# Sparse stage of the sample group: which input positions share a product, the order in which gathered rows lie, and when the value weights and the last pairs' chains are taken

## The reference, cut to what matters

```python
def compress_blocks(kv, pos_emb, w1, w2):
    # block i covers rows [i*16, i*16+32)
    hid = silu(einsum('nilgd,ldf->nigf', blocks + pos_emb, w1))   # 32 rows x 64 -> 256
    return einsum('nigf,fd->nigd', hid, w2)
...
# the compressed probabilities, summed over heads, choose the blocks
o = gates[..., 0] * o_cmp + gates[..., 1] * o_sel + gates[..., 2] * o_win
```

## Time and profile before

| | |
|---|---|
| median of 3 runs | 1810.35 us (1809.63 to 1811.09) |
| the profiled execution's own time | 1798.39 us |
| its span, first to last instruction | 1796.4 us |
| mean granted TensorE clock | 0.983 |
| the stage's PE products (L3329) | 980.2 us to 1253.9 us |

### The profile page before, as it was taken

How to read it: one execution, slowest core, us unless ns; L and a number is a source line. 1 busy time by engine, 2 the same in 40 slices (tenths; PEclk the granted TensorE clock), 3 DMA queues, 4 the chain that set the end, 5 groups by cost and what they waited for, 6 DMA issues and landing times. The chain is left out here.

```text
span 1796.4 us, 35438 instructions
## 1 busy us (share of the span) xinstructions
PE 1707.8 (95%) x13591; PEld 1427.7 (79%) x13591; DVE 964.7 (54%) x2741; ACT 732.3 (41%) x1582; POOL 425.8 (24%) x597
## 2 busy tenths in 40 slices
PE   7999999899898999999998987999799999999998
PEld 6778878678775878877788876988688888888998
DVE  5322222387455545221225878777587877778534
ACT  5200000276332424000112435445687777787513
POOL 0000000000464000000004434231365656565300
PEclk9999999999999999999999998999899999999999
DMA  6353343464888675575336434346400000000254
GB/s 222 133 176 135 140 170 110 159 210 126 288 248 269 241 249 174 134 201 184 131 108 207 150 119 129 125 148 167 119 20 26 26 25 20 25 14 8 58 161 156
DMA packets 150973, 247.47 MB, mean 138 GB/s; under 512 B 35451, under 2 KB 85368, under 8 KB 148504
## 3 DMA queue, kind: packets, MB, share of 16 engines
q1 hardware_dynamic: 135496, 200.58, 34.7%
q0 software_dynamic: 7424, 33.56, 5.4%
q10 hardware_dynamic: 7888, 11.08, 2.2%
...
## 5 line engine op out<-in xcount | busy, mean ns | idle before, releaser
L2000 POOL TENSOR_SCALAR sparse_pr<-sparse_pr,sparse_coef,sparse_gate 128x63 f32<-128x63 f32 (+8 forms) x384 | 246.8, 666 | 162.4 <-DVE sparse_coef L1940 162.4
L1886 ACT ACTIVATE sparse_pr<-sparse_pr,sparse_nmax 128x63 f32<-128x63 f32 (+8 forms) x384 | 227.7, 595 | 69.0 <-DVE sparse_nmax L1934 68.8
L1247 PE MATMUL x_acc<-x_w_hi,x_y_lo 128*128 128x512 f32 (+3 forms) x448 | 157.2, 351 | 1.7 <-DVE x_y_lo L1059 1.5
L1247 PE MATMUL x_acc<-x_w_lo,x_y_hi 128*128 128x512 f32 (+3 forms) x448 | 155.3, 347 | 0.0
L1247 PE MATMUL x_acc<-x_w_hi,x_y_hi 128*128 128x512 f32 (+3 forms) x448 | 155.0, 346 | 0.0
L512 PE MATMUL h_acc<-h_w_hi,h_y_lo 128*128 128x512 f32 x384 | 151.7, 395 | 0.8 <-DVE h_y_lo L434 0.8
L512 PE MATMUL h_acc<-h_w_lo,h_y_hi 128*128 128x512 f32 x384 | 150.1, 391 | 0.0
L512 PE MATMUL h_acc<-h_w_hi,h_y_hi 128*128 128x512 f32 x384 | 149.8, 390 | 0.0
L459 DVE COPY cmp_w<-h_acc 128x512 f32<-128x512 f32 x48 | 33.2, 691 | 204.7 <-PE h_acc L512 204.7
L1807 PE MATMUL sparse_ps<-cmp_lent,ss_pieces 64*128 64x384 f32 (+3 forms) x928 | 138.6, 427 | 3.9 <-DVE sparse_part L1934 2.2
L1819 PE MATMUL sparse_ps<-constants_shared,sparse_pr 128*128 128x128 f32 x1120 | 132.8, 276 | 3.4 <-DVE sparse_nmax L1934 2.3
...
## 6 DMA issues: line engine op xcount, KB each, us to landing
...
```

Of the source, the lines that this page charges most:

```text
L1247: last = nc.tensor.matmul(acc[b][:, 0:passes[p][3]], left[:, k, t * P:(t + 1) * P], weights(right, p)[:, k, :], start=(k == 0 and a == 0), ...
L1886: nc.scalar.activation(row, row, ACT.Exp, scale=-1.0, bias=nmax[u % UB][:, e * NBR + br:e * NBR + br + 1], accum_out=lsum[u % UB][:, e * N ...
L2000: nc.gpsimd.tensor_scalar(row, row, one, gate[:, t, 2 * i + e, (br + 1) % 3:(br + 1) % 3 + 1], ALU.mult, ALU.mult).then_inc(scaled, 1)
```

## The change

It does five things.

1. `SHARED` is steps 0 to 5 rather than 1 to 6, so an item begins with shared steps and ends with the two others; the first slot of an item forms the `ps_x` products first and waits for the addition to `ps_h[0]` behind them, and the wait for `ps_h[1]` stands behind three more.
2. Within 32 partitions the quarter gather now brings the rows of even positions first, then those of odd ones. The transposes of `turn_x` then write runs of 16 neighbouring values instead of alternating between the even and the odd half of the row. The index table is loaded by 8 small DMAs for each part instead of 4.
3. Value weights: the ring has 2 buffers with a third column block for the sum, so that POOL's sum waits for no cut; the parts are taken at slots 3, 5, 8, 10, 13, 15 of item 3 and 2, 4 of item 4, before at 3, 5, ..., 15 and (4,1); the sums of parts 0 and 1 are made in item 2.
4. The chains of pair 2 hang 4 slots earlier, those of pair 3 8 slots earlier; "cmp" of the pairs starts at (1,3), (2,4), (4,3), (5,8), before at (1,3), (2,4), (4,4), (6,4). In each chain "psel", "pwin", "values" and "acc" stand one slot later behind "scale" than before.
5. At the start of the stage DVE prepares step 0 behind the low part of the summed weights and the queries, before ahead of them.

```diff
-    SHARED = (1, 2, 3, 4, 5, 6)
-    RING_W = 3
+    SHARED = (0, 1, 2, 3, 4, 5)
+    RING_W = 2
...
     for p in range(PAIRS):
+        moved = max(0, p - 1) * 4
+
+        def slot(n, hh):
+            return divmod(n * HALVES + hh - moved, HALVES)
         e, o = 2 * p, 2 * p + 1
...
-        cmp_item, c0 = (o, 3) if p == 0 else (e, 4)
+        n, c0 = ((1, 3), (2, 4), (4, 3), (5, 8))[p]
...
+        for x, what in enumerate(("mask", "exp", "coef", "scale")):
+            at(*slot(o, tail + x), what, p)
         for x in range(2):
-            turn_at(*later(6), "psel", p, x)
-            turn_at(*later(7), "psel", p, 2 + x)
-        turn_at(*later(8), "pwin", p, 0)
-        turn_at(*later(8), "pnew", p, 0)
-        at(*later(10), "values", p)
-        at(*later(11), "acc", p)
+            turn_at(*slot(o, tail + 7), "psel", p, x)
+            turn_at(*slot(o, tail + 8), "psel", p, 2 + x)
+        turn_at(*slot(o, tail + 9), "pwin", p, 0)
+        turn_at(*slot(o, tail + 9), "pnew", p, 0)
+        at(*slot(o, tail + 11), "values", p)
+        at(*slot(o, tail + 12), "acc", p)
...
+    def weights_turn(n, hh):
+        at = [3 + 5 * l // 2 for l in range(KD)]
+        x = (n - PAIRS + 1) * HALVES + hh
+        return at.index(x) if x in at else None
...
-                last = nc.vector.transpose(to.rearrange("p r (n j) -> p n j r", n=8), fr.rearrange("p q g d -> p g q d"))
+                last = nc.vector.transpose(to.rearrange("p r (n j) -> p n r j", n=8), fr.rearrange("p q g d -> p g q d"))
...
-                    if sum_at(l):
-                        pool.wait_ge(next_cut, SHARED[sum_at(l) - 1] + 1)
-                    nc.gpsimd.tensor_tensor(w_next_sum[:, :], w_next[l % RING_W][:, 0, :], w_next[l % RING_W][:, 1, :], ALU.add).then_inc(next_summed, 1)
+                    nc.gpsimd.tensor_tensor(w_next[l % RING_W][:, 2, :], w_next[l % RING_W][:, 0, :], w_next[l % RING_W][:, 1, :], ALU.add).then_inc(next_summed, 1)
...
-                    if n == PAIRS - 1 and hh >= 2 and hh % 2 == 0 and shared(hh // 2 - 1):
-                        next_sum(hh // 2 - 1)
+                    if n == PAIRS - 2 and hh < RING_W and shared(hh):
+                        next_sum(hh)
+                    l = weights_turn(n, hh + 1)
+                    if l is not None and l >= RING_W and shared(l):
+                        next_sum(l)
...
+                    if first and not second:
+                        if n:
+                            pe.wait_ge(both_taken, n)
+                        for c in range(2):
+                            product(ps_x[:, c * XP:(c + 1) * XP], *both_halves(c), 0, start=c == 0)
+                        if n:
+                            pe.wait_ge(summed, 2 * n - 1)
...
+                        product(ps_h[0][:, 0:XP], *half(0, 0), XP, start=True)
+                        return
                     if first:
+                        product(ps_h[0][:, XP:2 * XP], *half(1, 0), 2 * XP)
                         if n:
-                            pe.wait_ge(summed, 2 * n - 1 + second)
+                            pe.wait_ge(summed, 2 * n)
```

More of the change, by code:

```diff
@@ L106, in _constants @@
     put("overlap", np.clip(over, 0, None) / 32.0)
-    put("sub", np.stack([p % 8, 4 * (p % 8) + p // 32], 1))
+    put("sub", np.stack([p % 8, 4 * (2 * (p % 4) + p % 32 // 16) + p // 32], 1))
     close(g)
@@ L2846, in load_table @@
                          allow_slow_non_contiguous=True).then_inc(self.table_in, 16)
-        for k in range(4):
-            at = 32 * part + 8 * k
-            sp.dma_start(self.quarters[at:at + 8, :, :],
-                         self.page_table.rearrange("n (q k) -> k n q", k=4)[k].unsqueeze(0).broadcast_to([8, NB, 4]),
+        for r, k in itertools.product(range(2), range(4)):
+            at = 32 * part + 16 * r + 4 * k
+            sp.dma_start(self.quarters[at:at + 4, :, :],
+                         self.page_table.rearrange("n (q k) -> k n q", k=4)[k].unsqueeze(0).broadcast_to([4, NB, 4]),
                          allow_slow_non_contiguous=True).then_inc(self.table_in, 16)
     def index(self, dve):
-        dve.wait_ge(self.table_in, 16 * (2 * PAST // PAGE + 1))
+        dve.wait_ge(self.table_in, 16 * (3 * PAST // PAGE + 1))
         self.nc.vector.tensor_copy(self.pages_f[:, :], self.pages[:, :]).then_inc(self.index_step, 1)
@@ L3014, in attend_samples_sparse @@
         w_sum = comp.lent[:, 0:len(SHARED) * CH].rearrange("p (l f) -> p l f", l=len(SHARED))
-        w_next = [sb(f"w_next{b}", [P, 2, CH]) for b in range(RING_W)]
-        w_next_sum = sb("w_next_sum", [P, CH])
+        w_next = [sb(f"w_next{b}", [P, 3, CH]) for b in range(RING_W)]
         x_hi, x_lo = ([sb(f"{n}{b}", [P, 3 * XP], F32R) for b in range(N_X)] for n in ("x_hi", "x_lo"))
@@ L3343, in hidden @@
                         pe.wait_ge(x_cut, t + 1)
+                    if first and not second:
[5 more added lines that the diff above has]
+                            pe.wait_ge(summed, 2 * n - 1)
+                        else:
+                            pe.wait_ge(p_active, 4)
+                        product(ps_h[0][:, 0:XP], *half(0, 0), XP, start=True)
+                        return
                     if first:
+                        product(ps_h[0][:, XP:2 * XP], *half(1, 0), 2 * XP)
                         if n:
-                            pe.wait_ge(summed, 2 * n - 1 + second)
-                        elif not second:
-                            pe.wait_ge(p_active, 4)
+                            pe.wait_ge(summed, 2 * n)
+                        product(ps_h[1][:, 0:XP], *half(0, 1), XP, start=True)
+                        product(ps_h[1][:, XP:2 * XP], *half(1, 1), 2 * XP).then_inc(x_used, 1)
+                        return
                     if not shared(l):
                         even, odd = ps_h[second][:, 0:XP], ps_h[second][:, XP:2 * XP]
-                        product(even, *half(0, second), 0, start=first)
+                        product(even, *half(0, second), 0)
                         product(even, *half(1, second), XO_AT)
@@ L3360, in hidden @@
                     if not second:
-                        if l == SHARED[0] and n:
-                            pe.wait_ge(both_taken, n)
                         for c in range(2):
-                            last = product(ps_x[:, c * XP:(c + 1) * XP], *both_halves(c), 0, start=l == SHARED[0] and c == 0, stop=l == SHARED[-1] and c == 1)
+                            last = product(ps_x[:, c * XP:(c + 1) * XP], *both_halves(c), 0, stop=l == SHARED[-1] and c == 1)
                         if l == SHARED[-1]:
@@ L3566, in other_work @@
                         take_x_high(act, step_ahead(n, hh))
-                    if (n, hh) == (PAIRS, 1) or n == PAIRS - 1 and hh >= 3 and hh % 2 == 1:
-                        next_high_part(KD - 1 if n == PAIRS else (hh - 3) // 2)
+                    if weights_turn(n, hh) is not None:
+                        next_high_part(weights_turn(n, hh))
                     for what, p, *x in events(n, hh):
@@ L3721, in other_work @@
                         take_x_low(dve, step_ahead(n, hh))
-                    if (n, hh) == (PAIRS, 1) or n == PAIRS - 1 and hh >= 3 and hh % 2 == 1:
-                        next_low_part(KD - 1 if n == PAIRS else (hh - 3) // 2)
+                    if weights_turn(n, hh) is not None:
+                        next_low_part(weights_turn(n, hh))
                     for what, p, *x in events(n, hh):
@@ L3776, in _ @@
                 last.then_inc(bank_free[nb], 1)
+                turn_x(dve, 0)
+                take_x_low(dve, 0)
                 for t in range(1, AHEAD):
```

59 lines of the change are left out of this document (27 added, 32 removed).

## The result

The changed kernel takes 1817.55 us (median of 7 runs, 1814.38 to 1819.14), the kernel before 1810.35 us (7 runs, 1809.63 to 1813.17). The ratio is 1.0036 with a 95% interval of 1.0027 to 1.0046: **slower by 0.36%**, where 8 us less were forecast. The profiled execution took 1814.38 us, its span is 1812.6 us.

The account below looks back on a forecast made before the run. PE, busy 95%, was taken as the bound, so only its waits and the slower clock behind them could shrink. Terms -2.1 - 3.7 - 1.9 - 2.9 + 2.0 - 0.7 + 1.3 = -8.0 us gave 1802.4 us, range 1787 to 1811 us.

Parts of the forecast that it names:

- Transposes: DVE's 256-column transposes fall from 630 ns to 0.40 us, a pair takes 0.70 us, saving 0.43 us in each of 64 steps.
- Start: Stage start: summed weights' low part and queries move into DVE's wait for the gather, first product at 978.0: -2.1 us.
- Item 0 to 1: First item boundary: DVE gets ahead of PE, so the 2.31 us wait and 1.4 us of clock go: -3.7 us.
- 1 to 2: Second item boundary: PE's wait for DVE's addition becomes 4.4 us instead of 6.31 us: -1.9 us; the clock still falls.
- Item 3 to 4: Boundary after item 3: coef 2.8 us later, addition ends at 23.0 instead of 21.3 us: +2.0 us, bounds -10 to +5.
- Gathers: Item 4: pair 2's keys, gathered at (4,3) and turned at (4,7), land late for PE: +1.3 us, up to +5.
- Scaling of pair 2: PE's other wait for POOL's scaling, 2.2 us, gets one slot more and no weights in between: -0.7 us.
- Tail: Stage end: pair 3's turns and values leave it but are PE's work in either place: zero, bounds -2 and +2.
- Other boundaries: Item boundaries 2 to 3, 4 to 5, 5 to 6, 6 to 7, holding 5.1 us of waits: -2.9 us.
- The stage's waits are the same program's, so I subtract there: Base of the forecast: the 8.0 us is taken from the runs' median 1810.35 us, not the profiled 1798.39 us.
- The first rival: Item 3's stall dissolves because coef comes early and ACT never waits for POOL's sum: -21 us, 1789 us; chance 20%.
- The last rival: Slower: item 3's chain decides, coef comes 9 us later, addition ends 12 us later: +6 us, 1816 us; chance 14%.

Follow-up runs that it names:

- e13: The changed kernel once more, on a chip of the quick kind: 1802.93 us against 1799.82 us for the kernel before, ratio 1.0012.
- e1: Kernel before with part 2 of the change alone (gathered row order, transposes in runs of 16, index table): 1790.57 us against 1802.37 us, ratio 0.9940.
- e15: The kernel of e1 once more, part 2 alone: 1790.19 us against 1799.82 us for the kernel before, ratio 0.9940.
- e16: The kernel before, unchanged, profiled again on e13's chip of the quick kind, where its median is 1799.82 us.
- e6: The kernel before, unchanged, profiled again on a chip with stalls, where its median is 1809.75 us.
- e18: Kernel of e9 with the chains of pairs 2 and 3 moved by 4 and 8 slots, psel to acc not later: 1790.71 us, ratio 0.9938.
- e17: Kernel of e9 with the chain of pair 2 alone moved by 4 slots: 1784.06 us, 0.9904 of the kernel before.
- e12: Kernel before with parts 1, 2 and 5 of the change, value weights and chains as before: 1793.30 us, ratio 0.9963.
- e9: Kernel of e12 with value weights' parts at slots 3, 5, 7, 9 of items 3 and 4: 1786.43 us, 0.9928 of the kernel before.
- e10: Changed kernel with value weights' parts at slots 3, 5, 7, 9 of items 3 and 4, ring of three: 1792.89 us, 0.9967 of the kernel before.

## Why the prediction was wrong, point by point

The forecast was -8.0 us in the stage. On a chip of the quick kind it came out at +4.9 us in the profile (e13; +3.1 us by the medians). By stretches, forecast and e13: up to the first product -2.1 and -1.0 us, from there to (3,8) -6.3 and -5.2 us, to (5,8) +2.6 and +4.9 us, to the end -2.2 and +6.2 us. The 13 us between lie as follows.

- *Transposes: right for one, 0.414 us where 0.40 us was said; too good for the pair.* The sum took 0.70 us for two; they take 0.80 us to the next instruction (978.49 to 979.30 us), so a step saves 0.33 us and not 0.43 us. Their share was too small all the same: with slow transposes the forecast would have been 6 us less, and e1 and e15 give 10 to 12 us. The slower clock behind the waits, counted only for item 0 to 1, may be what was missing; e1 fits that and e15 doesn't.
- *Start: -2.1 us predicted, -1.0 us in e13 and -0.4 us in the profile shown.* Next to e16, the kernel before on e13's chip, e13 is 0.4 us earlier. From transposes to product it took 3.9 us, 3.6 us was predicted. But the transposes began 38.1 us behind the cast instead of 36.6 us. The subtraction for the summed weights was put into "DVE's wait for the gather", and that wait has POOL's work behind it: the gather at 970.19 took 1.74 us beside the subtraction of 969.36, its like before took 0.95 us. The six runs with the old start order have 0.94 or 0.95 us for this gather, the fourteen with the new one 1.74 or 1.75 us. That is 0.8 us; the rest of the 1.5 us lies in the landing, which varies in the kernel before as well (transposes at 36.05 us in e16, 37.25 us in e6). The Trainium skill, SBUF — State Buffer, "SBUF: two separate sides", says that DVE with two SBUF inputs and a GpSimd operation that reads SBUF lock each other out of a shared pair of ports for a whole instruction; its warning of gathers whose descriptors can't be written speaks of DVE's two-port performance modes, not of such a subtraction. The trace fits the lock, for an operation that the warning does not name: the gather ends 971.93 - 971.12 = 0.81 us behind the subtraction, about what it takes alone.
- *Item 0 to 1 and 1 to 2: mechanisms right, size too large.* In e13 the wait for the addition is gone at the first boundary, and the second is 4.50 us where 4.4 us was said. From the first product to (3,8) the gain is 5.2 us, of which 0.7 us is the order of the steps, so 4.5 us are left; -3.7 - 1.9 and the share of 2 to 3 promised 6.3 us. e1 alone has 5.2 us there, without any help of the order: what the first slot saves at (2,0), 5.4 - 4.5 = 0.9 us, is not kept. That ps_x products ahead of the addition only move the wait is a reading that no run isolates.
- *Item 3 to 4: right chain, size too small.* Predicted: coef at 11.5 us behind the window scores, the addition's end at 23.0 us, PE idle 10 us or more, +2.0 us. Measured in the profile shown, from the window scores at 1105.19 us: coef 1117.64 - 1105.19 = 12.4 us, the addition's end 1129.23 - 1105.19 = 24.0 us, PE idle 3.88 + 6.81 = 10.7 us. From (3,8) to (5,8), where the keys' gather (+1.3 predicted) lies as well, e13 loses 4.9 us; with the share of boundary 4 to 5 the forecast had +2.6 us. All of it is waiting: PE is idle 14.1 us there against 9.2 us before, and busy 66.2 us against 66.1 us.
- *Gathers: right.* 1.9 us of waiting for pair 2's keys in the profile shown, 1.6 us in e13, where +1.3 us was said.
- *Scaling of pair 2: right in its wait* (4.2 - 3.9 = 0.3 us left of 2.2), and wrong in what follows: the wait moved to the copies of the turned probabilities (0.95 us for ACT's and 1.10 us for DVE's, two slots later).
- **The step that failed is "Tail ... Zero, bounds -2 and +2", together with "Other boundaries ... -2.9".** From (5,8) to the end e13 loses 6.2 us, where these steps and the scaling gave -2.2 us, or -1.5 us with the 0.7 us for the order of the steps: 8 of the 13 us lie here. What failed is "They are PE's work in either place": the tail was weighed as if the place that pair 3's chain goes to were free. e18 against e17 shows the price by itself: 4.9 us for pair 3's move in the stage, 6.7 us by the medians. At the tail the balance was about right (2.0 us of waits against 2.4 us). The cost is in item 7, where pair 3's exponential, scaling and copies now hold what PE waits for, 3.2 us against 0.6 us, and in PE's slower clock at the end. "Other boundaries" gained nothing here either: with no chain moved, e12 loses 0.5 us in this stretch (0.7 us of it is the order of the steps) where e1 wins 1.1 us. Some of e13's 6.2 us is chance: the same kernel's profile shown loses 4.0 us here and is 2.7 us at the low level, e13 9.0 us.
- *The 4 us between +3.1 us on the quick kind of chip and the +7.2 us of the first comparison are the chip.* The changed kernel loses 16 us to the stalls, the kernel before 10. "The stage's waits are the same program's, so I subtract there" was the wrong step: the base of 1810.35 us contains stalls of which the rows show nothing.

The first rival named something that exists. With the parts taken away from the boundary the stall of item 3 shrinks, and e9 and e10 are 7 and 8 us faster; but the changed kernel's own turns put a part there again. The last rival asked for a coef 9 us late; it was 3.8 us late, and the kernel was slower by other waits.
